# A two-layer decoder trunk: token-major first norm, query norm inside the softmax scale, later spreads and additions

## The chip, the cores and the metric

The kernel runs on one core of one Trainium2 chip. The metric is the device time of one execution in microseconds. Five engines work side by side: PE (TensorE, matrix products), DVE (VectorE), ACT (ScalarE), POOL (GpSimd) and SP, which here only issues DMAs. Each runs its own instructions in program order, and they wait for one another by semaphores.

## The reference

272 tokens (16 meta tokens and 256 inputs) of 1024 numbers go through two layers; all is float32.

```
h = rms_norm(r, g1);  proj = h @ w_in        # q_lat 384 | kv_lat 256 | k_pe 32 | dq | dk | dv 512 each | gates 2 x 1024
# branch A, 8 heads
c_q = rms_norm(q_lat);   q = c_q @ w_uq      # per head 64 + 32, rotary on the 32
c_kv = rms_norm(kv_lat); k, v = c_kv @ w_ukv # per head 64 + 64; k gets rotary(k_pe), 32, shared
out_a = (softmax(q k^T / sqrt(96), causal) v) @ w_o_mla
# branch B, 4 heads, two maps each, rotary on the first 16 of 64
p = softmax(q1 k1^T / 8) - lam * softmax(q2 k2^T / 8)   # lam from exp of two sums of products
out_b = rms_norm(p v) * (1 - lam_init) @ w_o_diff
r = r + rms_norm((sigmoid(g_a) * out_a + sigmoid(g_b) * out_b) @ w_out)
r = r + rms_norm((silu(gu[:2816]) * gu[2816:]) @ w_down),  gu = rms_norm(r) @ w_gate_up
```

The output is the residual stream without the meta tokens. A `rms_norm` divides by a root over a token's numbers, so its factor is one number per token and can be multiplied in after the matrix product.

## The kernel before, in words

Activations lie with features on the 128 partitions and tokens along the free axis, as 8 chunks of 128 x 272. Each float32 product is made of three: a value is split into a high part (a cast to fp32r, on ACT) and a low part (value minus high part, on DVE), and PE multiplies high by high, high by low and low by high. The inputs' chunks are `hh` and `hl`, the weights `w_hi` and `w_lo`.

Weights come as 252 slots of 128 x 1024 (512 KB) in the order of use. SP's `load` fills a ring of 4 raw slots, and waits for the low part of slot n - 4 before it loads slot n. ACT's `split` casts a raw slot into a ring of 8 high parts, DVE's `split` (L718) subtracts into a ring of 8 low parts. ACT runs 7 slots ahead of the tile that an instruction order is at, DVE 6. PE's `tile` does 24 matmuls for an output tile of 128 features (8 chunks x 3) into one of the PSUM banks: six up to the middle of the ukv tiles, four behind them. `bank_free` makes it wait until the tile that had the bank before is evacuated, which DVE counts in `tile_free`.

The order of every engine is written out by hand. In a layer, PE makes the latent tiles `lat` (6), `dq` and `dk` (4 each), then in turn the query tiles `uq` (6 short ones), `dv` (4) and key and value tiles `ukv` (8 short ones), then 16 `gate` tiles, between which the attention of 12 heads (units) stands, then `oa`, `ob`, `out`, the FFN's `gu` and `down`. After gate tile 2 come `keys_ready` and, in layer 0, `meta_rows` (the scores of the meta tokens); inside gate tile 3 the first scores; behind gate tile 4 the first `transposes` of probabilities.

A norm is done in steps. ACT squares chunk by chunk, POOL adds, PE's `norm_sums` multiply by a column of ones, ACT's `root` takes the root, DVE's `recip` the reciprocal, and PE's `spread` transposes the column of factors into rows across all partitions, from where DVE's `take` (L731) copies them. The first norm is squared from x while the first two slots are split in quarters (`quarter_split`), and its spread stands inside tile lat 3. The latents' norms are spread inside tile dk 1 (`latent_spreads`). The query norm's factors are multiplied in when DVE evacuates the uq tiles: with the rotary tables (`rcos_q`, `rsin_q`) for the rotary part, directly (L926) for the rest.

Rotary parts are two products, one of them moved along the partitions by a shuffle, and added on POOL (`rope_add`: 0 the shared key, 1 dq, 2 dk, 3 uq). ACT copies the rotary part of the queries into place (L468, "placing"). DVE makes the masks in bf16 and the product and sum for lambda after tile lat 3; ACT's exp and DVE's `lambdas` follow. `keep_clock` issues small matmuls on idle data, 50 of them at the start.

## Time and profile before

| | us |
|---|---|
| median of 3 runs (lowest, highest) | 828.0 (827.8, 829.01) |
| the profiled execution | 828.09 |
| its span | 826.1 |
| PE, DVE, ACT, POOL busy | 812.8, 590.5, 451.5, 128.8 |

The span runs from the first to the last instruction that the profile shows; what the profiled execution took beside it lies around it. Matmuls are pipelined, so PE's busy time includes the time in which one matmul's end overlaps the next one's start: the distance from start to start tells more than the duration.

### The profile page before, as it was taken

Reading aid. Unit: us, or ns where it says so; the run is one execution under the profiler, and the core shown is the slowest. Engines: PE = TensorE matmul, PEld = TensorE weight load, DVE = VectorE, ACT = ScalarE, POOL = GpSimd, SP = SyncE. Lnnn points to the kernel's source line nnn. Section 1 sums busy time; section 2 is a strip of 40 time slices with the busy share of each in tenths; the row PEclk is TensorE's granted clock in tenths of the full one; section 3 lists DMA queues with packets and bytes.
Section 4 is the critical chain, followed back from the end, with each engine's and each line's share of the span. In section 5 each row is a group of like instructions: output and inputs, shape, how many; then the busy total and the mean of one; then the engine's idle time right before and its main releaser. Section 6 shows DMA issues by size and latency. Waiting matters only on the chain.

```text
span 826.1 us, 17079 instructions
## 1 busy us (share of the span) xinstructions
PE 812.8 (98%) x6437; PEld 789.2 (96%) x6437; DVE 590.5 (71%) x1000; ACT 451.5 (55%) x749; POOL 128.8 (16%) x128
## 2 busy tenths in 40 slices
PE   8999999999999999999999999999999999999997
PEld 8999999999999999999999999899999999999885
DVE  4999586569588666666668996876787876766432
ACT  6755555475566444455556547554766655545431
POOL 2122000004341111101113220000054211111000
PEclk9999999999999999999999999999999999999999
DMA  7666523235527656446662666233363566555631
GB/s 288 215 193 203 158 78 103 80 100 182 176 74 251 182 159 180 129 144 186 178 201 81 202 196 210 80 102 102 105 229 102 184 226 188 182 189 177 205 102 51
DMA packets 38747, 131.59 MB, mean 159 GB/s; under 512 B 4384, under 2 KB 4768, under 8 KB 38688
## 3 DMA queue, kind: packets, MB, share of 16 engines
q1 hardware_dynamic: 38688, 130.77, 50.3%
q8 instruction: 42, 0.69, 0.3%
q14 instruction: 17, 0.14, 0.1%
HBM read 129.70 MB, written 1.05 MB: 158 GB/s over the span
## 4 chain that ended last, share of the span: by engine, by line
PE 81%; DVE 12%; ACT 2%; issue 2%; DMA 2%; POOL 0%; SPq 0%; DVEq 0%; POOLq 0%; ACTq 0%
PE bank L1147 20%; PE bank L1149 19%; PE bank L1148 19%; DVE w_lo L718 5%; PE bank L1183 4%; PE bank L1505 2%; PE bank L1506 2%; PE bank L1504 2%; PE bank L1172 2%; PE bank L1375 2%; DMA w_raw<-weights 2%; PE bank L1351 2%; PE bank L1390 1%; PE bank L1199 1%; ACT e_t L491 1%
## 5 line engine op out<-in xcount | busy, mean ns | idle before, releaser
L718 DVE TENSOR_TENSOR w_lo<-w_raw,w_hi 128x1024 fp32r<-128x1024 f32 x250 | 337.2, 1351 | 38.4 <-ACT w_hi L362 36.2
L1147 PE MATMUL bank<-h_hi,w_hi 128*128 128x272 f32 (+1 forms) x1232 | 357.8, 290 | 0.0
L1149 PE MATMUL bank<-h_hi,w_lo 128*128 128x272 f32 (+1 forms) x1232 | 352.0, 286 | 0.0
L1148 PE MATMUL bank<-h_lo,w_hi 128*128 128x272 f32 (+1 forms) x1232 | 351.2, 285 | 0.0
L362 ACT ACTIVATE w_hi<-w_raw 128x1024 fp32r<-128x1024 f32 x250 | 262.4, 1054 | 125.0 <-PE bank L1149 53.9
L1147 PEld LDWEIGHTS bank<-h_hi,w_hi 128*128 128x128 f32 x1232 | 232.0, 188 | 1.3 <-issue 0.2
L1149 PEld LDWEIGHTS bank<-h_hi,w_lo 128*128 128x128 f32 x1232 | 231.8, 188 | 0.0
L1148 PEld LDWEIGHTS bank<-h_lo,w_hi 128*128 128x128 f32 x1232 | 231.6, 188 | 0.0
L642 POOL TENSOR_TENSOR acc<-acc,sq 128x272 f32<-128x272 f32 (+1 forms) x51 | 52.5, 1029 | 143.6 <-ACT sq L375 143.1
L687 POOL TENSOR_TENSOR pbuf<-sbuf,ubuf 128x272 f32<-128x272 f32 (+1 forms) x44 | 38.7, 878 | 205.4 <-DVE ubuf L1081 203.8
L1081 DVE TENSOR_TENSOR ubuf<-bank,rstd_h 128x272 f32<-128x272 f32 (+1 forms) x44 | 18.9, 431 | 45.2 <-PE bank L1149 45.2
L1147 PE MATMUL bank<-ff_hi,w_hi 128*128 128x272 f32 x176 | 50.7, 288 | 0.0
L1149 PE MATMUL bank<-ff_hi,w_lo 128*128 128x272 f32 x176 | 50.6, 288 | 0.0
L1148 PE MATMUL bank<-ff_lo,w_hi 128*128 128x272 f32 x176 | 50.6, 287 | 0.0
L675 POOL TENSOR_TENSOR gates<-gates 128x272 f32<-128x272 f32 (+1 forms) x16 | 15.7, 1005 | 208.9 <-DVE gates L736 208.9
L591 ACT ACTIVATE sbuf<-gbuf 128x272 f32<-128x272 f32 (+1 forms) x44 | 18.7, 424 | 51.3 <-DVE gbuf L1081 51.0
L491 ACT ACTIVATE e_t<-bank,small 128x272 f32<-128x272 f32 x64 | 27.1, 431 | 31.0 <-DVE small L945 31.0
L1183 PE MATMUL bank<-h_hi,w_hi 128*128 128x272 f32 (+1 forms) x144 | 38.1, 293 | 2.8 <-DVE w_lo L787 2.4
L1183 PE MATMUL bank<-h_hi,w_lo 128*128 128x272 f32 (+1 forms) x144 | 37.7, 290 | 0.0
L1505 PE MATMUL bank<-w_lo,ff_hi 128*128 128x512 f32 x88 | 34.7, 395 | 0.0
L1506 PE MATMUL bank<-w_hi,ff_lo 128*128 128x512 f32 x88 | 34.7, 394 | 0.0
L1504 PE MATMUL bank<-w_hi,ff_hi 128*128 128x512 f32 x88 | 34.6, 394 | 0.0
(211 smaller groups left out, 1238.1 us busy)
## 6 DMA issues: line engine op xcount, KB each, us to landing
w_raw<-weights SPq DMA_DIRECT2D x220, 512.0 KB, 3.7
w_raw<-weights SPq DMA_DIRECT2D x16, 384.0 KB, 3.1
w_raw<-weights SPq DMA_DIRECT2D x16, 320.0 KB, 2.8
resid<-x_t SPq DMA_DIRECT2D x4, 272.0 KB, 5.3
out_tokens<-o_tok SPq DMA_DIRECT2D x4, 256.0 KB, 2.0
cst<-consts SPq DMA_DIRECT2D x1, 544.0 KB, 6.2
gain_bc<-gain_rows SPq DMA_DIRECT2D x1, 512.0 KB, 4.3
y<-consts SPq DMA_DIRECT2D x1, 256.0 KB, 5.8
```

Of the source, the lines that this page charges most:

```text
L362: act.activation(w_hi[:, n % RING, :], w_raw[:, n % RAW, :], ACT.Copy).then_inc(hi_ready, 1)
L491: last = act.activation(e_t[:, e, a:b], ps[bank][:, a:b], ACT.Exp, bias=mx[u % 2][:, s + part:s + part + 1], scale=scale, accum_out=sm[u % ...
L642: pool.tensor_tensor(acc[:, K % 2, t0:], acc[:, K % 2, t0:], sq[:, plan.sq_place[K, c], t0:], ALU.add).then_inc(sq_added, 1)
L687: pool.tensor_tensor(pbuf[:, j % 2, t0:], sbuf_[:, j % 2, t0:], ubuf[:, j % 2, t0:], ALU.mult).then_inc(ff_prod, 1)
L718: dve.tensor_tensor(w_lo[:, n % RING, :], w_raw[:, n % RAW, :], w_hi[:, n % RING, :].bitcast(f32), ALU.subtract).then_inc(lo_ready, 1)
L1147: pe.matmul(dst, wh, hi, start=first, stop=False)
L1148: pe.matmul(dst, wh, lo, start=False, stop=False)
L1149: return pe.matmul(dst, wl, hi, start=False, stop=last)
L1183: pe.matmul(ps[bank_of(t)][:, t0:TOK], w[:, n % RING, k * P:(k + 1) * P], src[k][0], start=k == 0 and q == 0, stop=False)
L1504: pe.matmul(dst, x_hi, wh, start=k == 0, stop=False)
L1505: pe.matmul(dst, x_hi, wl, start=False, stop=False)
L1506: return pe.matmul(dst, x_lo, wh, start=False, stop=k == FC - 1)
```

## The change

What it does, part by part:

- **First norm.** x is also passed token by token (`x_rows`). ACT squares and sums each token's row in one instruction with an accumulator, takes the root over 3 columns, and DVE the reciprocal; PE only spreads it (`first_spread`), inside tile lat 5. The 8 squares, POOL's additions and PE's 12 sums of this norm go.
- **First weights and inputs.** Slots 0 to 3 arrive in a buffer of their own in 5 pieces (by chunks of rows: 1, 1, 2, 2, 2), between the pieces of x; the gains come inside the first one. ACT and DVE split piece by piece. PE makes four tiles at once (`start_tiles`), per piece high by high, high by low input, low weights. 40 warm-up matmuls instead of 50. The first slot that waits for a ring place on SP is slot 8.
- **Query norm.** Its factor is no longer multiplied into the queries nor spread by PE. As it is a number per query, it goes into the softmax scale: `pscale` and `nscale`, a column each, in ACT's exp and DVE's negative maximum. ACT instead of DVE evacuates uq tiles 2 to 5, as plain copies.
- **Latent spread.** Only the key and value norm is spread, in tile dk 3 instead of dk 1.
- **Rotary additions.** `rope_add` 2 and 3 on POOL wait for the last ukv tile. ACT places the queries after the second v copy (gate tile 1) and not between the dv tiles.
- **Masks and lambda.** The casts of the masks go to POOL, at its start. Lambda's product and sum come at gate tile 0, exp at 1, `lambdas` at 3 (layer 0).

The diff, cut to its core:

```diff
@@ SP
+            for i, (a, b) in enumerate(PIECES):
+                if a % 2 == 0:
+                    xs = slice(GAIN_COLS + a * TOK if a else 0, GAIN_COLS + (a + 2) * TOK)
+                    sp.dma_start(x_sb[:, xs], xT[:, xs]).then_inc(x_in[a // 2], 16)
+                ws = slice(FIRST * P * a, FIRST * P * b)
+                sp.dma_start(w_first[:, ws], first_weights[:, ws]).then_inc(piece_in[i], 16)
+            load(4, SLOT)
+            load(5, SLOT)
             sp.dma_start(cst[:, 0:P], consts[:, 0:P]).then_inc(id_in, 16)
+            sp.dma_start(x_tok[:, 0:2, :], x_rows[:, 0:2 * D_MODEL].rearrange("p (c d) -> p c d", c=2)).then_inc(rows_in, 16)
+            sp.dma_start(x_tok[0:N_META, 2, :], x_rows[0:N_META, 2 * D_MODEL:]).then_inc(rows_in, 16)
+            load(6, SLOT)
...
@@ ACT
             first_hi(0, 1)
+            piece_split(0)
+            piece_split(1)
             first_hi(2, 3)
+            piece_split(2)
             first_hi(4, 5)
+            piece_split(3)
             first_hi(6, 7)
+            piece_split(4)
+            split(FIRST)
+            split(FIRST + 1)
+            act.wait_ge(rows_in, 32)
+            for c, (a, b) in enumerate(KEYS):
+                n = b - a
+                act.activation(x_sq[0:n, c, :], x_tok[0:n, c, :], ACT.Square, accum_out=x_sum[0:n, c:c + 1]).then_inc(row_squared, 1)
+            act.wait_ge(row_squared, len(KEYS))
+            act.activation(std[0][:, 0:len(KEYS)], x_sum, ACT.Sqrt, bias=eps, scale=1.0 / D_MODEL).then_inc(norm_std, 1)
...
                 for st, i in TURNS:
                     split(S(st, i) + HI_AHEAD)
-                    if (st, i) == ("dv", 2):
-                        act.wait_ge(rope_done, 4 * (l + 1))
-                        for q in range(4):
-                            act.activation(q_t[64:96, q::4, t0:], q_rot[32 * q:32 * q + 32, :, t0:], ACT.Copy).then_inc(q_placed, 1)
+                    if st == "uq" and i >= 1:
+                        for j in (2 * i, 2 * i + 1):
+                            t, h = TL("uq", j), 2 * j - 4
+                            act.wait_ge(pe_done, plan.tile_done[t])
+                            act.activation(q_t[0:NOPE, h, t0:], ps[bank_of(t)][0:NOPE, t0:TOK], ACT.Copy)
+                            act.activation(q_t[0:NOPE, h + 1, t0:], ps[bank_of(t)][NOPE:, t0:TOK], ACT.Copy).then_inc(act_free, 1)
...
                         if i < 3:
                             v_evac(i)
+                            if i == 1:
+                                act.wait_ge(rope_done, 4 * (l + 1))
+                                for q in range(4):
+                                    act.activation(q_t[64:96, q::4, t0:], q_rot[32 * q:32 * q + 32, :, t0:], ACT.Copy).then_inc(q_placed, 1)
+                            if i == 1 and l == 0:
+                                act.wait_ge(lam_ready, 1)
+                                act.activation(lam_e, lamp, ACT.Exp).then_inc(lam_exp, 1)
@@ POOL
-            sum_squares(0, 0)
+            pool.wait_ge(id_in, 16)
+            pool.wait_ge(mask_in, 16)
+            pool.wait_ge(pe_done, plan.tile_done[0])
+            pool.tensor_copy(identb[:, :], ident)
+            pool.tensor_copy(maskb[:, :], stage[:, 0, 0:P])
+            pool.tensor_copy(maskmb[:, 0:128], stage[0:16, 0, 128:256])
+            pool.tensor_copy(maskmb[:, 128:256], stage[0:16, 1, 0:128]).then_inc(const_ready, 1)
...
                 rope_add(l, 1, dqk[:, 0:4, t0:], rot["dq"][:, :, t0:])
+                pool.wait_ge(pe_done, plan.tile_done[plan.tile[l, "ukv", MLA_HEADS - 1]])
                 rope_add(l, 2, dqk[:, 4:8, :], rot["dk"])
                 rope_add(l, 3, q_rot[:, :, t0:], rot["uq"][:, :, t0:])
@@ DVE
+            for i, (a, b) in enumerate(PIECES):
+                dve.wait_ge(x_in[a // 2], 16)
+                for c in range(a, b):
+                    lo_part(0, c, G_MIXPRE, 0, 0)
+                piece_split(i)
+            split(FIRST)
+            split(FIRST + 1)
             recip(PRE_MIX, 0)
             take(PRE_MIX, 7, rstd_h, 0)
...
                         if st == "dq" and i == 3:
                             recip(K0 + NQ, t0)
+                            query_scales(K0 + NQ, len(token_chunks(t0)))
                             recip(K0 + NKV, 0)
-                        if st == "dk" and i == 1:
-                            take(K0 + NQ, 7, rstd_q, t0)
+                        if st == "dk" and i == 3:
                             take(K0 + NKV, 6, rstd_kv, 0)
-                            v = step(dve.tensor_tensor(rc_q[:, t0:], rstd_q[:, t0:], cos_m[:, t0:], ALU.mult))
-                            v = step(dve.tensor_tensor(rs_q[:, t0:], rstd_q[:, t0:], sin_m[:, t0:], ALU.mult))
...
-                        dve.tensor_scalar(mx[u % 2][:, s:s + 2], mx[u % 2][:, s:s + 2], -scale, None, ALU.mult).then_inc(negmax_ready, 1)
+                            dve.tensor_tensor(mx[u % 2][:, s:s + 2], mx[u % 2][:, s:s + 2], nscale, ALU.mult).then_inc(negmax_ready, 1)
...
                         split(S("gate") + i + AHEAD)
+                        if i == 0 and l == 0:
+                            lambda_sums()
                         if i == 3 and l == 0:
+                            lambdas()
@@ PE
+            def start_tiles(src):
+                for i, (a, b) in enumerate(PIECES):
+                    for k in range(a, b):
+                        pe.wait_ge(h_hi, k + 1)
...
+                            pe.wait_ge(piece_hi, i + 1)
+                        for t in range(FIRST):
+                            pe.matmul(ps[t][:, :TOK], w_hi[:, t, k * P:(k + 1) * P], src[k][0], start=k == 0, stop=False)
+                    for k in range(a, b):
+                        pe.wait_ge(h_lo, k + 1)
+                        for t in range(FIRST):
+                            pe.matmul(ps[t][:, :TOK], w_hi[:, t, k * P:(k + 1) * P], src[k][1], start=False, stop=False)
...
+                        pe.wait_ge(piece_lo, i + 1)
+                    for k in range(a, b):
+                        for t in range(FIRST):
+                            mm = pe.matmul(ps[t][:, :TOK], w_lo[:, t, k * P:(k + 1) * P], src[k][0], start=False, stop=k == KC - 1)
...
-            keep_clock(50)
+            keep_clock(40)
...
+                first_norm = {4: first_spread} if l == 0 else {0: lambda: norm_sums(K0 + PRE_MIX, 7, 0), 4: lambda: norm_spread(K0 + PRE_MIX, 7, 0)}
                 for i in range(4, 6):
                     slot_ready(S("lat") + i)
+                    tile(TL("lat") + i, S("lat") + i, 0, P if i < 5 else HW, full, 0, inside=first_norm if i == (4 if l else 5) else None)
                 def latent_spreads():
-                    norm_spread(K0 + NQ, 7, t0)
-                    norm_spread(K0 + NKV, 6, 0)
+                    pe.wait_ge(norm_rec, K0 + NKV + 1)
+                    spread(K0 + NKV, 6, 0, count=2)
...
-                        tile(TL(st) + i, S(st) + i, 0, P, src, c0, inside={6: latent_spreads} if (st, i) == ("dk", 1) else None)
+                        tile(TL(st) + i, S(st) + i, 0, P, src, c0, inside={6: latent_spreads} if (st, i) == ("dk", 3) else None)
```

Where a tile's evacuation was counted in `tile_free` alone, the counts are now kept per engine (`emptied`, with `act_free` for ACT's). Buffers move a little in SBUF; the computation is the same.

## Rows read from the trace of the kernel before

**Rows 1.** Page, part 1: busy us, share of the span, instructions.

```profile
...
PE 812.8 (98%) x6437; PEld 789.2 (96%) x6437; DVE 590.5 (71%) x1000; ACT 451.5 (55%) x749; POOL 128.8 (16%) x128
...
```

**Rows 2.** Timeline, all engines, start: start us, us, engine line op tiles, [idle before].

```profile
...
1.06 4.63 PE L1225 MATMUL bank<-identb 128*128 128x128 bf16 x50 [1.06 <-DVE identb L780]
...
4.11 0.93 ACT L401 ACTIVATE h_hi<-resid,gain 128x272 fp32r<-128x272 f32 x2 [1.87 <-DMA resid<-x_t]
...
6.70 1.15 ACT L407 ACTIVATE w_hi<-w_raw 128x512 fp32r<-128x512 f32 x2 [1.66 <-DMA w_raw<-weights]
...
8.11 0.60 PE L1183 MATMUL bank<-h_hi,w_hi 128*128 128x272 f32 x1 [2.42 <-DVE w_lo L787]
...
```

**Rows 3.** Windows: PE, PEld, DVE, ACT, POOL busy (instructions); granted clock; DMA share, GB/s.

```profile
...
4.60:8.00 3.40, 1.09 (x19) 0.92 (x17) 1.55 (x4) 1.74 (x5) 0.00 (x0) 1.00 1.01 318
8.00:11.40 3.40, 3.29 (x14) 3.29 (x15) 3.12 (x7) 3.40 (x9) 0.77 (x1) 0.50 1.04 407
22.00:86.00 64.00, 62.50 (x493) 61.65 (x493) 61.50 (x110) 40.13 (x53) 13.47 (x10) 1.00 0.67 205
...
```

**Rows 4.** Waits of PE, whole span: total us, times, longest.

```profile
...
PE bank L1218 <- DVE small L726: 2.4, 2, 1.2
...
```

**Rows 5.** Timeline of PE, four short stretches.

```profile
...
18.73 0.72 PE L1199 MATMUL bank<-small,acc 128*128 128x1 f32 x6
...
19.99 0.37 PE L1147 MATMUL bank<-h_hi,w_hi 128*128 128x272 f32 x1
...
23.55 0.29 PE L1147 MATMUL bank<-h_hi,w_hi 128*128 128x272 f32 x1
...
79.35 0.29 PE L1149 MATMUL bank<-h_hi,w_lo 128*128 128x272 f32 x1
79.94 0.36 PE L1147 MATMUL bank<-lat_hi,w_hi 128*128 128x272 f32 x1 [0.30 <-DVE kv_t L736]
...
499.48 0.28 PE L1149 MATMUL bank<-lat_hi,w_lo 128*128 128x272 f32 x1
499.90 0.39 PE L1147 MATMUL bank<-lat_hi,w_hi 128*128 128x272 f32 x1
...
```

**Rows 6.** Timeline of DVE, layer 0 up to the gates.

```profile
...
22.99 0.44 DVE L731 COPY rstd_h<-bank 128x272 f32<-128x272 f32 x1 [0.63 <-PE bank L1218]
...
32.55 0.21 DVE L805 CAST identb<-cst 128x128 bf16<-128x128 f32 x1
...
40.59 0.16 DVE L818 TENSOR_TENSOR small<-small 128x1 f32<-128x1 f32 x1
...
52.80 2.92 DVE L718 TENSOR_TENSOR w_lo<-w_raw,w_hi 128x1024 fp32r<-128x1024 f32 x1
...
69.84 0.43 DVE L926 TENSOR_TENSOR q_t<-bank,rstd_q 64x272 f32<-64x272 f32 x1
...
```

**Rows 7.** Timeline of POOL, layer 0 up to the gates.

```profile
...
51.30 3.34 POOL L651 TENSOR_TENSOR dqk_t<-dqk_t,b_t 128x1088 f32<-128x1088 f32 x1 [8.82 <-DVE b_t L897]
63.31 3.37 POOL L651 TENSOR_TENSOR dqk_t<-dqk_t,gates 128x1088 f32<-128x1088 f32 x1 [8.67 <-DVE gates L897]
68.98 2.17 POOL L651 TENSOR_TENSOR gates<-gates 128x544 f32<-128x544 f32 x1 [2.29 <-DVE gates L908]
...
```

**Rows 8.** Timeline of ACT, end of ukv and gates of layer 0.

```profile
...
74.85 2.70 ACT L468 ACTIVATE q_t<-gates 32x544 f32<-32x544 f32 x4
...
95.53 0.90 ACT L483 ACTIVATE v_tok<-bank 128x256 f32<-128x256 f32 x3 [2.23 <-PE bank L1307]
...
97.40 1.28 ACT L516 ACT_TABLE_LOAD   x1
...
```

**Rows 9.** Timelines of DVE (two rows) and PE, gates of layer 0.

```profile
...
96.94 0.41 DVE L990 TENSOR_REDUCE small<-bank 16x16 f32<-16x256 f32 x1 [0.69 <-PE bank L1329]
...
103.94 0.78 DVE L967 SCALAR_TENSOR_TENSOR e_t<-e_t,small 128x272 f32<-128x272 f32 x2
...
105.08 0.71 PE L1375 MATMUL bank<-cst,e_t 128*128 128x128 f32 x5
...
```

More of the change, by code:

```diff
@@ L129, in __init__ @@
         self.slots = len(self.slot_done)
+        self.emptied, counts = [], {}
+        for t, (l, name) in enumerate(self.name_of):
+            by = "act" if name == "uq" and t - self.tile[l, name, 0] >= 2 else "dve"
+            counts[by] = counts.get(by, 0) + 1
+            self.emptied.append((by, counts[by]))
         self.bank, self.before = [], []
@@ L150, in __init__ @@
             for k in range(NORMS):
-                if k in CHUNKS:
+                if k in CHUNKS and (l or k != PRE_MIX):
                     K = l * NORMS + k
@@ L158, in __init__, with build_trunk @@
                         self.sq_free[K, c] = users[-2] if len(users) >= 2 else None
-                        users.append(("sum", K + 1) if last else ("add", a))
+                        users.append(("sum", K) if last else ("add", a))
                     s += CHUNKS[k]
-def build_trunk(nc: bass.Bass, xT, weights, gains, lam_in, consts, gain_rows, out):
+def build_trunk(nc: bass.Bass, xT, x_rows, first_weights, weights, lam_in, consts, gain_rows, out):
     f32, f32r, bf16 = mybir.dt.float32, mybir.dt.float32r, mybir.dt.bfloat16
@@ L666, in _ @@
                 pool.wait_ge(rope_done, 4 * (l + 1))
-                pool.wait_ge(pe_done, plan.tile_done[plan.tile[l, "ukv", MLA_HEADS - 1]])
                 if l == 0:
@@ L1158, in tile, with first_tiles @@
                 mm.then_inc(pe_done, 1)
-            def first_tiles(tiles, ready, before=None):
+            def first_tiles(tiles, ready):
                 if tiles[0][1]:
@@ L1177, in first_tiles @@
                 for k in range(KC):
-                    if before and k in before:
-                        before[k]()
                     pe.wait_ge(hi_sem, base + k + 1)
@@ L1247, in _ @@
                 if l == 0:
-                    first_tiles([(TL("lat") + q, S("lat") + q, late, t0) for q in range(2)], (h_hi, h_lo, 0),
-                                {0: lambda: pe.wait_ge(quarter_lo, 1), 2: lambda: pe.wait_ge(quarter_lo, 2),
-                                 4: lambda: pe.wait_ge(quarter_lo, 3), 6: lambda: slot_ready(1)})
-                    slot_ready(S("lat") + 2)
-                    tile(TL("lat") + 2, S("lat") + 2, 0, P, late, t0)
-                    norm_sums(K0 + PRE_MIX, 7, 0)
-                    pe.wait_ge(id_in, 16)
-                    slot_ready(S("lat") + 3)
-                    tile(TL("lat") + 3, S("lat") + 3, 0, P, full, 0, inside={6: lambda: norm_spread(K0 + PRE_MIX, 7, 0)})
+                    start_tiles(full)
                 else:
@@ L1296, in v_transposes @@
                         pe.wait_ge(norm_ready, K0 + NKV + 1)
-                        pe.wait_ge(tile_free, TL("dv", 3) + 1)
+                        emptied(pe, TL("dv", 3))
+                        for b in range(BANKS, BANKS + EXTRA):
+                            emptied(pe, max(t for t in range(TL("gate")) if plan.bank[t] == b))
                     else:
-                        pe.wait_ge(tile_free, TL("ukv", 4 * g - 1) + 1)
+                        emptied(pe, TL("ukv", 4 * g - 1))
                         pe.wait_ge(v_copied, 9 * l + 3 * g)
@@ L1624 @@
     gain_rows = np.broadcast_to(A(norm_ffn_post)[DEPTH - 1][None, :], (P, D_MODEL))
-    arrays = {"x_t": x_t, "weights": packed, "gains": gains, "lam": lam, "consts": constants(), "gain_rows": gain_rows}
+    first = packed[0:FIRST * P].reshape(FIRST, P, SLOT)
+    first = np.concatenate([first[:, :, a * P:b * P].transpose(1, 0, 2).reshape(P, -1) for a, b in PIECES], axis=1)
+    arrays = {"x_t": x_t, "x_rows": x_rows, "first_weights": first, "weights": packed, "lam": lam, "consts": constants(), "gain_rows": gain_rows}
     arrays = {k: np.ascontiguousarray(v) for k, v in arrays.items()}
```

221 lines of the change are left out of this document (112 added, 109 removed).

## The prediction, made before the changed kernel ran

> **What bounds the kernel now.** I read the page first: PE is busy 812.8 of 826.1 us [rows 1]. A busy PE says little by itself, so I looked at what PE waits for and at the distance between its matmul starts: from 8.11 us on, matmuls of 272 columns start 0.125 us apart almost without a break. So time is won only where PE's stream starts earlier, waits less or gets shorter. There are three such places.
>
> The start: the warm-up matmuls are issued by 5.5 us, the first useful one runs at 8.11, after 2.42 us idle [rows 2]. Behind it the granted clock is 0.50, the 1.2 GHz level, from 8.0 to 11.4; in the stretch before, PE was busy 1.09 of 3.4 us [rows 3].
>
> The latent spread: PE waits 1.2 us twice, once a layer, for DVE's reciprocal [rows 4].
>
> The bank of a ukv tile: ukv 4 starts at 79.94, after 0.30 us of waiting for an evacuation by DVE [rows 5]. DVE is busy 61.5 of the 64 us from 22 to 86 [rows 3] and has fallen behind PE by then: it is second in line, and a gain of PE ahead of this point is worth nothing unless DVE gets shorter too.
>
> **The start.** The fourth tile ends and the fifth begins at 23.55 now [rows 5]. Call that moment E. Landings: x's first piece (272 KB behind 38 KB of gains) is there at 4.1, the first half of two slots (0.84 MB in all) at 6.7 [rows 2]; from 8.0 on 407 GB/s flow [rows 3]. By these, and with SP's first issue now x itself (0.3 us saved), 0.58 MB (x and piece 0) are there at 5.0, 0.84 at 6.35, 1.65 at 8.35, 2.45 at 10.35 and 3.25 MB (piece 4) at 12.3. To cast 512 columns takes ACT 0.6 us (two took 1.15 [rows 2]), 1024 take 1.05; with the h_hi casts between them the high parts end at 5.7, 7.0, 9.5, 11.5 and 13.4. PE has 12 matmuls for each of eight row chunks, 96 x 0.125 = 12.0 us. It starts at 5.75, runs chunks 0 and 1 to 8.75, waits 0.75 for piece 2, and then always has work: E = 5.75 + 12.0 + 0.75 = 18.5. The low part no longer stands ahead of the first matmul; DVE makes it in 0.65 us, while PE has 8 high matmuls. Gone are the cold stretch and the 12 column sums of the first norm with the wait at their end (18.73 to 19.99 [rows 5]). So E comes 5.05 us earlier. Bounds: 17.8 (no wait for pieces) and 20.5 (each landing 0.7 later, and the low clock once). The 10 warm-up matmuls that go end before PE could start, so they give nothing.
>
> The new norm: the token rows (1.1 MB) stand behind slots 4 and 5, 5.4 MB in all, so at some 17.6. Three squares on ACT at about 1.1 with their accumulator reads, and a root, give 21.6, the reciprocal 21.8. PE asks for it in the sixth tile, chunk 4, at E + 4.5 = 23.0: 1.2 to spare. A straggling DMA queue would use this up; bounds 0 and 1 us, I take 0.
>
> A new wait: slot 6's low part stands on DVE behind this later norm. Spread (0.33), copy and evacuation (0.35 each), and a split of 1.2 end at E + 7.1; PE is through the sixth tile at E + 6.3 and waits 0.8. Bounds 0.3 and 2.0 (the casts on POOL fall into it).
>
> **From there to ukv 4.** Now this takes 79.94 - 23.55 = 56.4 us. Off: the latent spread's wait 1.2 [rows 4], and 0.46 at ukv (79.35 to 79.94 less one pitch [rows 5]). The query norm's three transposes leave, the first norm's three come in. On: 0.8. So 55.5, if DVE keeps up. The spread itself: DVE's reciprocals come at E + 28.7, PE asks in dk 3, chunk 6, at E + 31.7; two tiles earlier it would wait.
>
> DVE's own sum: its chain began with the copy at 22.99 [rows 6], now at E + 5.0 = 23.5, 0.5 later. It loses four casts 0.55, the lambda product and sum 0.78, the lambda steps 1.26, the copy of the query factor 0.34, two rotary products 0.7, and eight query evacuations 3.7 (0.43 each and their gaps) [rows 6]: 7.3 us. Four small operations for the scales add 0.6. The evacuation that PE waited for would be ready at 79.9 + 0.5 - 6.7 = 73.7; PE arrives at 18.5 + 55.5 = 74.0. They meet. But a split in this chain took 2.92 instead of 1.2: it ended 1.1 behind the end of a POOL addition (51.30 + 3.34 [rows 6, 7]). The second addition, dk's at 63.31 [rows 7], held up another split by 1.0; it now runs after the last ukv tile. That puts DVE 1.3 us ahead.
>
> The Trainium skill, "SBUF — State Buffer", Who interferes with whom, has this as a lock: a DVE instruction with two SBUF inputs and a POOL one that reads SBUF exclude each other, and the first one holds it for its whole length. By that rule the trace agrees. It also speaks against the casts and additions on POOL, which by it may stand behind a split or hold up one.
>
> ACT takes the eight query copies (0.43 each, 3.4 us) and gives up the placings (2.70 [rows 8]), one exp and one sqrt table load (1.28 each) in this stretch, in which it is busy 40 of 64 us [rows 3]: nothing. The banks that they free are asked for six tiles later, 1.8 us to spare.
>
> So PE reaches ukv 4 at 74.0, 5.9 us earlier.
>
> **The gates of layer 0.** Here is a loss. In the old clock times: the last v copies run at 95.53 after 2.23 us idle [rows 8]; ahead of them now stand the four placings (2.7) and the exp of lambda with its table load (1.5). They end at 98.3, and the scores start at 98.5: just no wait. But ACT's split of that turn ends 4 us later, DVE's behind it at 98.6, then come the lambda steps (1.25), and the meta maxima start at 99.9 instead of 96.94 [rows 9]. The table load that held up the meta exp (97.40 [rows 8]) is done by then: 0.9 back. So the first probabilities, ready at 104.72 now, come 2.1 later; PE, which takes them up at 105.08 [rows 9], had 0.3 to spare. Loss 1.8; bounds 0.5 (DVE's split isn't late) and 2.6. POOL's two additions (3.37 and 2.17 [rows 7]) end at 88.8, ACT asks at 92.3: 3.5 to spare.
>
> **Layer 1.** Spread wait 1.2, two transposes 0.2, ukv wait 0.3 (499.48 to 499.90 less a pitch [rows 5]): 1.7 off. The placings sit between the v copies here too, and the scores start where the copies end: 0.1 on. What follows the gates, the FFNs and the tail are untouched and bound by PE; they move along.
>
> **Sum.** 5.9 - 1.8 + 1.7 - 0.1 = 5.7 us. The profiled execution took 828.09 (span 826.1 and 2.0 around it), the median of the three is 828.0, so they are one: 822.4 us.
>
> **Rivals.** A: the clock. If PE's gaps of 0.4 us before its start and of 0.75 at 8.8 bring back the 1.2 GHz level for as long as now, 3.4 us [rows 3], PE loses half of that, less what it idles anyway: 1.5, so 823.9. For it: a gap did so now. Against: that one was 2.42 us. The Trainium skill, "TensorE: Matmul & The Clock Gate", Part 1, says that activity releases the clock and idling takes it back.
>
> B: DVE or ACT sets the pace up to ukv. DVE's lead is 0 to 1.3 us, and it hangs on slot 6's late split and on ACT's order, in which a query copy waits behind a split that waits for a load. If they are 3 us short, PE gives back 3: 825.4.
>
> C: no loss at the gates, and the pieces land at their best: 5.7 + 1.8 + 0.7 = 8.2, 819.9.
>
> D, slower: POOL's additions between the last ukv tile and the keys. The attention of a layer now waits for a chain: 5.5 us of additions, then four placings of 2.7, in order on ACT. If splits and additions shut each other out so that the additions end 7.5 us later than alone (13 for 5.5), the 3.5 to spare are used up and PE waits 4 in each layer: 822.4 + 8.0 = 830.4. It makes the kernel slower from a wait of 2.9 per layer on. For it: the split of 2.92. Against: one split of 1.2 ahead of each addition is only 2.4 of the 3.5.
>
> **Chances.** The forecast (821 to 823.4) 0.50, A 0.14, B 0.17, C 0.12, D 0.05, no change at all 0.02. The range is 819.4 (C with half a microsecond more) to 825.9 (B and a late norm). A measurement tells 0.2%, 1.7 us, from no change, so faster is under 826.3: forecast, A and C are faster, B mostly. Faster 0.87, same 0.08, slower 0.05.
>
> **What would show it.** The first useful matmul at 5.7 to 6.0 and the clock at 1.00 from there; the fifth tile at 18.5; a new wait of 0.8 for a low part before dq 0; no wait at the latent spreads; no doubled split beside the dk addition; ukv 4 at 74; a wait of about 1.8 before the first transposes of layer 0, with the meta maxima late. The forecast is wrong if the fifth tile starts after 20.5, if PE waits for key or query placings, or if over 3 us of PE waits appear between dq 0 and the first transposes.

## The result and the profile after

| | before | after |
|---|---|---|
| median of 6 runs each (lowest, highest) | 828.3 (827.8, 829.01) | 821.98 (821.15, 822.15) |
| the profiled execution | 828.09 | 822.15 |
| its span | 826.1 | 820.4 |

The ratio of the two is 0.9923, with a 95% interval from 0.9913 to 0.9933: the kernel became 0.8% faster, 0.4 us away from the forecast of 822.4. The profiled execution after is the slowest of its six. In the tables below "after" is the median of 821.98. The same kernel before, timed again beside each group of experiments, gave 828.08 to 828.18, so the groups can be set against each other.

The page and the windows of after, which answer to [rows 1, 3]. Columns of the windows: busy time (instructions) of each engine, then granted clock, DMA share, GB/s.

```profile
PE 809.3 (99%) x6410; PEld 786.1 (96%) x6410; DVE 583.9 (71%) x981; ACT 459.1 (56%) x760; POOL 122.3 (15%) x126
```

```profile
4.60:8.00 3.40, 3.40 (x25) 3.21 (x24) 2.42 (x5) 2.19 (x5) 0.00 (x0) 1.00 0.95 333
8.00:11.40 3.40, 2.40 (x19) 2.20 (x19) 1.99 (x4) 2.36 (x5) 0.00 (x0) 1.00 1.03 409
22.00:86.00 64.00, 63.14 (x506) 62.41 (x505) 59.04 (x95) 41.19 (x61) 13.72 (x14) 1.00 0.67 216
```

From 8.0 to 11.4 us the granted clock is 1.00 where it was 0.50, and PE works from 4.6 to 8.0 where it was idle for 2.42 us [rows 2, 3]. (The clock's record begins at 6.59 us in this trace, and the view counts what lies ahead of it as 1.00; the last section comes back to this.) DVE has 59.0 us of work in the 64 where it had 61.5. What PE waits for in the whole execution (total, times, longest):

```profile
PE bank L1439 <- DVE e_t L1004: 1.4, 4, 0.6
PE bank L1295 <- DVE identb L820: 1.1, 1, 1.1
PE bank L1237 <- ACT w_hi L430: 1.0, 1, 1.0
PE bank L1187 <- DVE w_lo L757: 0.6, 1, 0.6
PE bank L1405 <- DVE pm L1043: 0.6, 1, 0.6
PE bank L1187 <- DVE gates L775: 0.2, 1, 0.2
```

The two waits for DVE's `small` [rows 4] are gone. New are one for the first pieces (L1237), one for a low part (L1187), one for a bank in the query tiles (L1187, `gates`), one for the meta probabilities (L1405), and 0.65 of the 1.4 us at L1439. These are gaps between matmuls; from start to start, less the usual 0.125, a wait comes out 0.1 to 0.2 us longer, and the text counts it so: 1.17, 0.80, 0.38 and, at the gates, 0.65 and 0.8. PE's timeline shows their places:

```profile
1.09 4.45 PE L1295 MATMUL bank<-identb 128*128 128x128 bf16 x40 [1.09 <-DVE identb L820]
5.49 1.24 PE L1237 MATMUL bank<-h_hi,w_hi 128*128 128x272 f32 x4
6.53 0.69 PE L1241 MATMUL bank<-h_lo,w_hi 128*128 128x272 f32 x4
...
10.25 1.00 PE L1237 MATMUL bank<-h_hi,w_hi 128*128 128x272 f32 x6 [1.00 <-ACT w_hi L430]
...
19.37 0.29 PE L1187 MATMUL bank<-h_hi,w_hi 128*128 128x272 f32 x1
...
26.53 0.39 PE L1187 MATMUL bank<-h_hi,w_hi 128*128 128x272 f32 x1 [0.64 <-DVE w_lo L757]
...
74.97 0.29 PE L1187 MATMUL bank<-lat_hi,w_hi 128*128 128x272 f32 x1
...
97.62 0.76 PE L1405 MATMUL bank<-cst,pm 16*16 16x16 f32 x24 [0.57 <-DVE pm L1043]
...
101.48 0.77 PE L1439 MATMUL bank<-cst,e_t 128*128 128x128 f32 x5 [0.65 <-DVE e_t L1004]
```

Where PE stands against before (the first matmul of each place):

| place in PE's order | before | after | earlier by |
|---|---|---|---|
| fifth tile (E) [rows 5] | 23.55 | 19.37 | 4.18 |
| ukv 4 [rows 5] | 79.94 | 74.97 | 4.97 |
| first probabilities of layer 0 [rows 9] | 105.08 | 101.48 | 3.60 |
| start of layer 0's FFN | 225.78 | 221.77 | 4.01 |
| start of layer 1 | 430.36 | 426.44 | 3.92 |
| start of layer 1's FFN | 631.95 | 625.82 | 6.13 |
| first matmul of 512 columns | 759.23 | 753.11 | 6.12 |
| the end of the span | 826.1 | 820.4 | 5.7 |

### The profile page after: what moved, and what is told of

Read it like the earlier page. It is cut to its first block, busy times and chain, and to the rows that moved or that the text cites. A ratio compares the mean times of both kernels' runs of the same rounds, so it can differ in the third digit from the quotient of the medians.

```text
span 820.4 us, 17023 instructions
## 1 busy us (share of the span) xinstructions
PE 809.3 (99%) x6410; PEld 786.1 (96%) x6410; DVE 583.9 (71%) x981; ACT 459.1 (56%) x760; POOL 122.3 (15%) x126
## 4 chain that ended last, share of the span: by engine, by line
PE 90%; DVE 6%; ACT 2%; issue 1%; DMA 1%; SPq 0%; POOL 0%; DVEq 0%; POOLq 0%
PE bank L1187 22%; PE bank L1189 22%; PE bank L1188 22%; PE bank L1221 4%; PE bank L1568 3%; PE bank L1570 2%; PE bank L1569 2%; DVE w_lo L757 2%; PE bank L1212 2%; PE bank L1439 2%; PE bank L1415 1%; PE bank L1454 1%; PE bank L1269 1%; ACT e_t L515 1%; DMA w_first<-first_weights 1%
## 5 line engine op out<-in xcount | busy, mean ns | idle before, releaser
L1187 PE MATMUL bank<-h_hi,w_hi 128*128 128x272 f32 (+2 forms) x1216 | 353.1, 290 | 0.6 <-DVE w_lo L757 0.6
L1189 PE MATMUL bank<-h_hi,w_lo 128*128 128x272 f32 (+2 forms) x1216 | 347.4, 286 | 0.0
L1188 PE MATMUL bank<-h_lo,w_hi 128*128 128x272 f32 (+2 forms) x1216 | 346.6, 285 | 0.0
L1187 PEld LDWEIGHTS bank<-h_hi,w_hi 128*128 128x128 f32 (+1 forms) x1216 | 229.0, 188 | 1.9 <-DVE w_lo L757 0.9
L1189 PEld LDWEIGHTS bank<-h_hi,w_lo 128*128 128x128 f32 (+1 forms) x1216 | 228.8, 188 | 0.0
L1188 PEld LDWEIGHTS bank<-h_lo,w_hi 128*128 128x128 f32 (+1 forms) x1216 | 228.7, 188 | 0.0
L674 POOL TENSOR_TENSOR acc<-acc,sq 128x272 f32<-128x272 f32 (+1 forms) x45 | 46.9, 1042 | 124.7 <-ACT sq L399 124.7
L1187 PE MATMUL bank<-ff_hi,w_hi 128*128 128x272 f32 x176 | 50.7, 288 | 0.0
L515 ACT ACTIVATE e_t<-bank,small 128x272 f32<-128x272 f32 x64 | 30.0, 476 | 29.9 <-DVE small L982 18.2
L1187 PEld LDWEIGHTS bank<-ff_hi,w_hi 128*128 128x128 f32 x176 | 33.2, 189 | 0.0
L1188 PEld LDWEIGHTS bank<-ff_lo,w_hi 128*128 128x128 f32 x176 | 33.2, 188 | 0.0
```

What stands on the lines that cost most here:

```text
L515: last = act.activation(e_t[:, e, a:b], ps[bank][:, a:b], ACT.Exp, bias=mx[u % 2][:, s + part:s + part + 1], scale=scale, accum_out=sm[u % ...
L674: pool.tensor_tensor(acc[:, K % 2, t0:], acc[:, K % 2, t0:], sq[:, plan.sq_place[K, c], t0:], ALU.add).then_inc(sq_added, 1)
L1187: pe.matmul(dst, wh, hi, start=first, stop=False)
L1188: pe.matmul(dst, wh, lo, start=False, stop=False)
L1189: return pe.matmul(dst, wl, hi, start=False, stop=last)
```

## The experiments

Each was made from the changed kernel by the edit shown. Times are medians, with the lowest and highest run behind them.

| run | us | against after |
|---|---|---|
| spread_dk1 | 828.92 (828.05 to 830.95) | +6.9 |
| two_halves | 827.47 (825.86 to 828.76) | +5.5 |
| halves_warm50 | 827.75 (826.49 to 828.13) | +5.8 |
| halves_spread_dk1 | 835.31 (834.75 to 836.59) | +13.3 |
| norm_by_chunks | 824.47 (823.97 to 826.93) | +2.5 |
| uq_on_dve | 824.37 (823.55 to 824.58) | +2.4 |
| adds_early | 822.89 (822.28 to 823.09) | +0.9 |
| adds_place_early | 822.64 (822.19 to 823.01) | +0.7 |
| slot6_early | 822.05 (821.22 to 822.88) | +0.1 |
| warm50 | 821.83 (821.70 to 822.18) | -0.2 |
| gates_and_slot6 | 820.62 (820.14 to 821.20) | -1.4 |
| gates_order | 820.14 (819.87 to 822.70) | -1.8 |

### The latent spread: spread_dk1

```diff
-inside={6: latent_spreads} if (st, i) == ("dk", 3) else None
+inside={6: latent_spreads} if (st, i) == ("dk", 1) else None
```

(and DVE's `take` of it with it.)

> The changed kernel, with only the latent spread put back from tile dk 3 to tile dk 1 in both layers. My theory: the earlier start and the later spread need each other. In layer 0 PE now asks in dk 1, chunk 6, at about 45.4 us, and DVE's second reciprocal is ready at 49.4: a wait of 4.0. In layer 1 it is 1.3 as before the change. PE is the bound behind it, so nothing is given back: 5 us slower than the changed kernel, 827.0 (826 to 828). Rival: DVE is second in line, so while PE waits DVE catches up and the waits of 0.4 at uq and 1.5 at the gates shrink or go: 3.5 slower, 825.5. Second rival: the spread's move hides nothing that matters, under 1 us: 822.5.

Measured: 828.92, ratio to before 1.0007 (0.9996 to 1.0018). This edit alone takes back all of the gain, more than my theory or a rival said. PE's longest waits, its timeline at the spread, and the windows around it:

```profile
PE bank L1288 <- DVE small L765: 5.5, 2, 3.8
```

```profile
44.60 0.29 PE L1189 MATMUL bank<-h_hi,w_lo 128*128 128x272 f32 x1
48.73 0.54 PE L1288 MATMUL bank<-cst,small 128*128 128x128 f32 x3 [3.84 <-DVE small L765]
...
49.48 0.43 PE L1187 MATMUL bank<-h_hi,w_hi 128*128 128x272 f32 x1
49.71 0.43 PE L1188 MATMUL bank<-h_lo,w_hi 128*128 128x272 f32 x1
```

```profile
44.00:48.60 4.60, 0.89 (x8) 0.67 (x6) 4.57 (x14) 3.03 (x4) 0.00 (x0) 1.00 0.84 245
48.60:53.00 4.40, 4.27 (x22) 4.27 (x23) 4.40 (x7) 3.25 (x4) 2.76 (x1) 0.61 0.65 192
```

PE idles 4.0 us in layer 0 and 1.85 in layer 1. Behind the first wait matmuls start 0.23 us apart instead of 0.125, at the 1.2 GHz level, for 3.4 us: that costs another 1.5. Waits further down (0.38 before the uq tiles) go in exchange. Together 7.0; between the profiled executions it is 6.3, as this one's fifth tile starts 0.64 earlier (18.73). In layer 1 the wait was 1.33 before the change, and why it is 0.5 longer now stays open: the first norm of that layer wasn't touched.

### The start: two_halves, and both together

```diff
-PIECES = [(0, 1), (1, 2), (2, 4), (4, 6), (6, 8)]
+PIECES = [(0, 4), (4, 8)]
```

(the casts follow the pieces.)

> The first weight stage and the input are fetched in two halves of four chunks again, with the casts on ScalarE and VectorE half by half, and the matmuls in two rounds; the rest stays as changed. My theory: the first useful matmul comes at about 8.1 us instead of 5.5 and the end of the fifth tile at about 23.2 instead of 19.4, and, with the spread late, all of that goes through to the end: 825.9 us (824.8 to 827.0). Rival (the later start is taken up by the waits behind it, since VectorE's norm then is ready earlier against TensorE and the waits at 25.6 and in the gates go too): 823.5 to 824.7. Second rival (the pieces are worth nothing, all is the spread and the norm): 822.0 to 822.5.

Measured: 827.47; the profiled run was the lowest, 825.86. ScalarE's timeline there, and in halves_warm50, a profiled run of the common kind:

```profile
6.97 1.91 ACT L430 ACTIVATE w_hi<-w_first 128x2048 fp32r<-128x2048 f32 x1 [1.51 <-DMA w_first<-first_weights]
```

```profile
9.31 1.91 ACT L430 ACTIVATE w_hi<-w_first 128x2048 fp32r<-128x2048 f32 x1 [3.77 <-DMA w_first<-first_weights]
```

The trace's landing records show why they differ: 15 of the 16 DMA engines had brought the first 1 MB by 6.93 us in one and by 7.02 in the other; the sixteenth came at 6.95 and at 9.29. In the profiled run everything behind the start is the changed kernel's, 3.8 us later (the fifth tile starts at 23.15 instead of 19.37, the matmul behind the wait for slot 6's low part at 30.30 instead of 26.53), and the span is 3.7 longer. So a microsecond at the start is one at the end, as my theory had it; the forecast of 825.9 held for that run but not for the median. The next run asks whether the clock is the cause.

```diff
-keep_clock(40)
+keep_clock(50)
```

> The two halves of the run two_halves, with 50 warm-up matmuls instead of 40, as the kernel before had. The profiled run of two_halves took 825.9 us, but most of its others 827.3 to 828.8. My theory: TensorE sits idle there for 3.8 us ahead of its first useful matmul, so in most runs the clock falls back for some us; ten more warm-up matmuls shorten the idle time to about 2.7 us, and the time is 825.9 us (825.2 to 827.0), with nearly all runs there. Rival (the idle time is still long enough, as in the kernel before, whose records show 0.50 from 8.0 to 11.4): 827.4 (827.0 to 828.2).

Measured: 827.75, all but one of 11 runs above 827. It is the rival's number, but the clock isn't what sets this run apart from the faster one. The late sixteenth engine makes PE idle 5.6 us, and the first matmuls then run at the 1.2 GHz level:

```profile
8.00:11.40 3.40, 0.03 (x1) 0.06 (x1) 0.14 (x1) 2.09 (x2) 0.00 (x0) 0.52 1.00 400
11.40:15.00 3.60, 3.60 (x16) 3.60 (x17) 3.60 (x5) 3.20 (x5) 0.00 (x0) 0.50 1.04 426
```

They did so in the profiled run of two_halves too, whose record of the clock begins only at 13.65 us: its first 16 matmuls take 3.8 us, as long as here.

```profile
9.03 3.96 PE L1234 MATMUL bank<-h_hi,w_hi 128*128 128x272 f32 x16 [3.50 <-ACT w_hi L430]
12.79 2.55 PE L1238 MATMUL bank<-h_lo,w_hi 128*128 128x272 f32 x16
```

PE works at that level for 4.6 us there (9.03 to 13.65) and for 3.6 here (11.37 to 14.98), so the clock costs about 2 us in both. What differs is when the first matmul starts, 9.03 and 11.37, and the fifth tile, 23.15 and 25.05: that is the late engine, and it covers the 1.76 us between the two executions. There is one trace of each, so whether it also made the other runs of two_halves long isn't shown.

The third has two_halves' and spread_dk1's edits together.

> Two halves at the start and the latent spread back in tile dk 1, both at once: the start is as late as before, the first norm is the new one. My theory: the later latent spread is needed because the first norm now is spread 4.4 us behind the end of the fifth tile instead of ahead of it, so that VectorE's chain stands some 5 us further behind TensorE than before, whatever the start; then TensorE waits 3 to 4 us for the reciprocals in layer 0 and 1.9 in layer 1 here too, and the time is 833.0 us (831.0 to 835.0), slower than the kernel before. Rival (the spread wait of 4.0 us in spread_dk1 came from the earlier start alone: VectorE's reciprocal comes at its own time, 48 to 50 us, and a start 3.8 us later takes the wait back to about 1): 828.5 us (827.5 to 830.0).

Measured: 835.31, ratio 1.0082 (1.0068 to 1.0096), slower than before, and 2.3 above what I expected. The wait is as long as in spread_dk1, though the fifth tile starts 7.3 us later (25.99):

```profile
PE bank L1285 <- DVE small L762: 5.6, 2, 3.9
```

The clock costs more here than in spread_dk1. PE's first matmul starts at 11.30, as in halves_warm50, and it runs at the 1.2 GHz level up to 17.10; behind the wait of 4.0 us the level is 0.50 until 61.48, twice as long as in spread_dk1, and costs 2.5 us instead of 1.5:

```profile
54.60:61.40 6.80, 5.38 (x24) 5.38 (x25) 6.77 (x15) 4.88 (x4) 3.30 (x1) 0.50 0.69 231
```

So the wait doesn't come from the early start. By the timelines it comes from the place of the first norm's spread; no run moved that spread alone. Before, it stood inside the fourth tile, and DVE's chain began with the copy at 22.99, 0.56 ahead of E [rows 5, 6]. Now it stands in the sixth, and DVE's chain begins here in the changed kernel, 5.06 behind E:

```profile
22.89 0.18 DVE L765 RECIPROCAL small<-small 128x3 f32<-128x3 f32 x1 [4.71 <-ACT small L452]
24.43 0.44 DVE L770 COPY rstd_h<-bank 128x272 f32<-128x272 f32 x1 [1.36 <-PE bank L1256]
...
48.65 0.17 DVE L765 RECIPROCAL small<-small 128x3 f32<-128x3 f32 x1
```

DVE's chain starts 5.6 us later against E than before, and has lost 2.6 us of work by then (four casts, lambda): 3.0, against a wait that grew by 2.6. In spread_dk1 PE reaches the spread 26.0 us behind E and goes on 30.0 behind it. Two tiles (6 us) later, where the change puts it, there is no wait.

### The first norm: norm_by_chunks, slot6_early, warm50

The first norm of before, in the changed kernel (edit cut to its core):

```diff
-            sp.dma_start(x_tok[:, 0:2, :], x_rows[...]).then_inc(rows_in, 16)
...
-                act.activation(x_sq[0:n, c, :], x_tok[0:n, c, :], ACT.Square, accum_out=x_sum[0:n, c:c + 1]).then_inc(row_squared, 1)
+            for c in range(KC):
+                square(0, c, r[:, c, :], 0)
+            root(0, 7, D_MODEL, 0)
...
+            sum_squares(0, 0)
```

> The first norm is that of the kernel before again (squares chunk by chunk on ScalarE, added on GpSimd, summed over the partitions by TensorE in tile 5, no token-major rows fetched); the fetch pieces, the later latent spread, the query norm in the softmax scale and the rest stay as changed. My theory: the three sums of TensorE come back (0.15 to 0.25 us) and the squares share ScalarE with the casts of the pieces, whose reciprocal then comes a little later or earlier than 22.9; 822.8 us (822.2 to 823.6), so that the token rows are worth 0.8 of the 6.3 us. Rival (the rows and their fetch of 4 KB per token compete with the pieces and delay the fifth tile): without them the pieces land earlier and the time is 821 to 821.8. Second rival (the norm comes late by chunks and TensorE waits at the first spread): 824.5 or more.

Measured: 824.47, by the second rival's number; 823.97 in the profiled run, 1.8 above that of after, and all of it stands ahead of 28.3 us (the matmul behind the wait for the low part starts there at 28.32 instead of 26.53). PE's matmuls from 12 to 30 us (busy, mean ns), POOL's chain, and the wait for it:

```profile
L1265 PE MATMUL bank<-small,sq 128*128 128x1 f32 x6 | 0.8, 250 | 0.0
L1265 PE MATMUL bank<-small,acc 128*128 128x1 f32 x6 | 0.8, 249 | 0.7 <-POOL acc L669 0.7
```

```profile
16.92 5.73 POOL L669 TENSOR_TENSOR acc<-acc,sq 128x272 f32<-128x272 f32 x6 [16.47 <-ACT sq L397]
```

12 sums at 0.11 from start to start are 1.3 us, and 0.9 is waited for POOL, whose last addition ends at 22.65; a fifth tile that starts 0.5 earlier (18.90) takes a part back. I had left the 12 sums out of that expectation's price, though not out of the prediction's.

```diff
             recip(PRE_MIX, 0)
+            split(AHEAD)
             take(PRE_MIX, 7, rstd_h, 0)
```

(and the same split leaves its old place, behind the first evacuation.)

> VectorE's low part of the first slot of the latent stage's second group is moved ahead of the first norm's take, right behind the reciprocal; one statement is moved, nothing else. My theory: the 0.80 us that TensorE waits for that low part at 25.60 goes, and as much as 0.2 comes in at the first spread, whose take now ends later: 821.4 us (821.1 to 821.8). Rival (VectorE's whole load sets the pace up to the keys' and values' first tile): the 0.8 us come again at the next low parts or at the normalized chunks, and the time is that of the changed kernel, 822.0 (821.8 to 822.3).

Measured: 822.05, the rival's number. The wait before dq 0 falls only from 0.80 to 0.38 us, as DVE's split now waits 0.77 us for ACT's high part, and 0.7 us come again as waits before a uq tile (0.52 at 63.09; 0.38 was there) and a ukv tile (0.55 at 71.28).

> 50 warm-up matmuls instead of 40, nothing else. By the prediction's step the ten end before TensorE could start anyway. But the trace of the changed kernel shows the 40 ending right at the first useful matmul (5.49 us), so ten more, at about 0.11 us each, push it back. My theory: first useful matmul at 6.6, but the wait for piece 2 at 8.9 swallows what comes before it; time 822.0 us (821.6 to 822.5). Rival (the matmuls up to there are then late against piece 2 by more than the wait): 823.0. Second rival (the full clock from the first matmul on is worth something, the first ones being 0.26 us apart now): 821.3.

Measured: 821.83, no change that can be told. Here the full clock came only at 6.61 us, so the ten more matmuls took 1.06 us and pushed the first useful one from 5.49 to 6.36. But the trace has a fifth tile that starts at 18.62 instead of 19.37, and this in the sixth:

```profile
6.36 0.86 PE L1237 MATMUL bank<-h_hi,w_hi 128*128 128x272 f32 x4
...
23.61 0.40 PE L1256 MATMUL bank<-cst,small 128*128 128x128 f32 x2 [0.30 <-DVE small L765]
```

Piece 2 landed at 8.17 instead of 9.03, and PE, which came 0.5 us later, found it there. That isn't the edit's doing: in adds_place_early, with 40 matmuls, piece 2 landed at 8.17 too and the fifth tile starts at 18.52. Of the 0.75 us gained 0.48 is waited at the first norm's spread, since the last token rows land no earlier (19.67, and 19.27 in the changed kernel). An earlier start than the changed kernel's is worth next to nothing as long as the norm isn't earlier too.

### DVE's reserve: uq_on_dve, adds_early, adds_place_early

```diff
-by = "act" if name == "uq" and t - self.tile[l, name, 0] >= 2 else "dve"
+by = "dve"
```

(and the eight copies with it.)

> The changed kernel, with the evacuation of query tiles 2 to 5 back on DVE (plain copies, no factor), in both layers. My theory: up to the ukv tiles DVE is as late as PE. Eight copies of 0.43 put 3.4 us back on it per layer; its reserve at ukv is some 1.5 to 2 us in the trace of the changed kernel (it idles 0.9 ahead of slot 26's split and 0.2 elsewhere). PE then waits 1.5 to 2.5 us for banks in uq and ukv in layer 0 and 0 to 1 in layer 1: 824.2 (823 to 825.5). Rival: DVE has real slack and ACT was no help: under 0.5 us, 822.2.

Measured: 824.37, as expected. The eight copies (3.4 us of DVE) return as waits of 2.0 us, the longest of them here, and none in layer 1:

```profile
PE bank L1187 <- DVE q_t L962: 0.9, 1, 0.9
```

```diff
-                pool.wait_ge(pe_done, plan.tile_done[plan.tile[l, "ukv", MLA_HEADS - 1]])
                 rope_add(l, 2, dqk[:, 4:8, :], rot["dk"])
                 rope_add(l, 3, q_rot[:, :, t0:], rot["uq"][:, :, t0:])
                 pool.wait_ge(rope_done, 4 * (l + 1))
+                pool.wait_ge(pe_done, plan.tile_done[plan.tile[l, "ukv", MLA_HEADS - 1]])
```

> The changed kernel, with the rotary additions of dk and uq on POOL back ahead of the last ukv tile, in both layers; the placing of the queries stays late. My theory: a split of DVE beside the dk addition doubles again (2.2 in place of 1.2) and takes 1.0 of DVE's reserve of about 1.5 before ukv, and the long split (2.68) and the long lambda product (1.57) beside the additions in gate tile 0 go, where DVE has time. So no change of time: 822.0 (821.6 to 822.6). Rival: DVE's reserve is used up and PE waits 1 us per layer: 823.5 to 824. Second rival: the additions in the gates hold up the chain to the keys, and it gets 1 us faster: 821.

Measured: 822.89, 0.9 above the changed kernel, where I expected none: the reserve was smaller than I took it for. There is a new wait of 0.79 us before a dv tile (66.14), as the addition now stands beside DVE's splits again (one took 2.17); the waits at the gates stay.

The fourth takes the placings back between the dv tiles as well.

> The changed kernel, with the additions of dk and uq as before the change and the four placings of the queries on ACT back between dv 2 and ukv, in both layers. My theory: the loss at the gates of layer 0 (waits of 0.65 ahead of the meta transposes and 0.8 ahead of the first transposes) comes from ACT's order: placings 2.7 and lambda's exp 1.5 ahead of the third split and v copy. Without the placings there, ACT and DVE reach the meta maxima 1.3 to 2.4 us earlier and the waits shrink to 0 to 0.3. On the other side ACT spends 2.7 more ahead of ukv, where a split of DVE waited 0.9 for it. Net 0.5 to 1.4 faster than the changed kernel: 821.0. Rival: the loss comes from DVE's lambda steps alone (1.25), so it stays: 822.0. Second rival: ACT is late at ukv and PE waits there: 823 or more.

Measured: 822.64, and not the gain that I expected. The waits at the gates, 0.65 and 0.8 us, do go, but 0.8 is waited before a dv tile (66.08) and 0.9 before a ukv tile (78.49) instead. Both additions and placings stand better where the change puts them.

### The gates of layer 0: gates_order, gates_and_slot6

ScalarE and VectorE in the changed kernel at the gates. The order is: placings, table load, exp of lambda, a split, the v copies; VectorE waits for that split, makes the lambda steps and only then the meta maxima (L1030).

```profile
87.32 2.70 ACT L542 ACTIVATE q_t<-gates 32x544 f32<-32x544 f32 x4
90.04 1.28 ACT L545 ACT_TABLE_LOAD   x1
91.33 0.20 ACT L545 ACTIVATE small<-small 128x4 f32<-128x4 f32 x1
91.44 1.04 ACT L386 ACTIVATE w_hi<-w_raw 128x1024 fp32r<-128x1024 f32 x1
```

```profile
92.52 1.23 DVE L757 TENSOR_TENSOR w_lo<-w_raw,w_hi 128x1024 fp32r<-128x1024 f32 x1 [2.46 <-ACT w_hi L386]
...
94.42 0.41 DVE L1030 TENSOR_REDUCE small<-bank 16x16 f32<-16x256 f32 x1
```

```diff
 ACT
-                        split(S("gate") + i + HI_AHEAD)
+                        if i < 3 or l:
+                            split(S("gate") + i + HI_AHEAD)
...
-                            if i == 1 and l == 0:
-                                act.wait_ge(lam_ready, 1)
-                                act.activation(lam_e, lamp, ACT.Exp).then_inc(lam_exp, 1)
...
+                            act.wait_ge(lam_ready, 1)
+                            act.activation(lam_e, lamp, ACT.Exp).then_inc(lam_exp, 1)
                             act.wait_ge(meta_shift, 1)
...
+                            split(S("gate") + i + HI_AHEAD)
 DVE
-                            lambdas()
...
+                            lambdas()
                             dve.wait_ge(meta_exp, 1)
```

> In layer 0's gates, the lambda exponential and the meta exponential stand on ScalarE ahead of its high-part copy of gate 3, and VectorE's lambda steps behind the shift of the meta scores; nothing else. My theory: in the changed kernel the two waits of TensorE there (0.65 and 0.8 us) hang on that order: VectorE's low part at 92.52 waits 2.46 us for ScalarE's high part, which stands behind the placings, the table load and the exponential, and the steps behind it push the meta probabilities back. With the order mended both go, and the time is 820.5 us (820.0 to 821.2), 1.5 below the changed kernel. Rival (VectorE's total sets the pace here, as the run with the placing brought forward hints): the waits come again in front of the first scores tile, 821.6 to 822.0. Second rival (the split, now later, holds the last gate): a wait of 1 to 2 us at gate tile 3, 823.

Measured: 820.14, ratio to before 0.9909 (0.9895 to 0.9923), four of five runs at or below 820.42. The split comes at 89.75 there, and the maxima 2.4 us earlier:

```profile
90.83 1.22 DVE L758 TENSOR_TENSOR w_lo<-w_raw,w_hi 128x1024 fp32r<-128x1024 f32 x1 [1.06 <-ACT w_hi L386]
91.98 0.40 DVE L1030 TENSOR_REDUCE small<-bank 16x16 f32<-16x256 f32 x1
```

Both waits are gone from PE's list: 1.45 of the 1.73 us between the two profiled executions. This is the best version of the study, though its interval and the changed kernel's still overlap; that the gain is real rests on the trace as well.

> The order of gates_order and the low part moved of slot6_early, both. My theory after those two runs: VectorE's total up to the last key and value tile sets when TensorE gets there, so the low part gives nothing by itself and nothing here: 820.2 us (819.8 to 820.8), the time of gates_order. Rival (with the gates mended a gain ahead of them is kept): 819.5.

Measured: 820.62. The low part gives nothing here either.

## Why the prediction was right, step by step

- **The start.** Forecast E = 18.5, measured 19.37. The first useful matmul ran at 5.49 (forecast 5.75), but the first four were 0.26 us apart; the two first pieces took 3.5 us and not 3.0. Piece 2 was there at 9.03 (forecast 8.35), and PE waited 1.17 us instead of 0.75. So the sum was 0.87 too good in this run. The slow first matmuls cost nothing by themselves, as PE waited for piece 2 behind them. In the other nine traces with five pieces the fifth tile starts at 18.52 to 19.20 and piece 2 lands at 8.17 to 8.85, so the forecast sits at the lower edge of what was measured.
- **The warm-up.** The prediction said that the ten matmuls less end before PE could start anyway. They would not have: 40 of them end at 5.54, with the first useful one at 5.49, and 50 end at 6.60 in warm50. It cost nothing, because the wait for piece 2 lies behind it.
- **The new norm.** The step that was wrong without showing in the time: the rows were there at 19.3, not 17.6, and the reciprocal at 22.89, not 21.8. By the landing records the 1 MB of the first 256 tokens was complete at 17.11, in time; what came at 19.27 were the last 16 rows, 64 KB behind it in the queue (17.61 and 18.94 in uq_on_dve). ACT waits for both. To fetch the 16 rows first wasn't tried. With E 0.87 late there was no wait (the spread stands at 23.90, the reciprocal ends at 23.07). With E at 18.5 the 1.2 us "to spare" would have been none, and PE would have waited here, as it does for 0.48 in warm50.
- **The wait before dq 0**: forecast 0.8, measured 0.80.
- **From E to ukv 4**: forecast 55.5, measured 55.60. No wait at the spread or at ukv, but 0.38 us before a uq tile (63.47), where the forecast had none. DVE's lead was judged well: no large wait, but no reserve either, as uq_on_dve, adds_early and slot6_early show. A split beside the dq addition took 2.86 us (1.22 alone), as before [rows 6, 7]; at gate tile 0 another took 2.68 beside dk's, where nothing waits for it.
- **What the late spread is worth.** The prediction counted 1.2 us a layer off and said that two tiles earlier PE would wait, but not how long: 4.0 and 1.85 us, and 1.5 for the clock. The part of the change that looks like 2.4 us is the one on which all of it hangs.
- **The gates of layer 0**: forecast a loss of 1.8 by way of ACT's late split, DVE's low part and the meta maxima. Measured 0.65 + 0.8 = 1.45 by that way; maxima at 94.42, by the forecast's clock 99.4 instead of 99.9. gates_order shows that it is this chain.
- **Layer 1**: forecast 1.6, measured 2.2 (from 3.92 to 6.13 earlier). A stall of 0.41 us at 117.31 in layer 0 went too, which the prediction had not seen. The tail gave 0.4 back: the 264 matmuls of 512 columns take 61.40 us from the first start to the last and not 61.02. They do so in the traces of all the variants, so it belongs to the change and isn't scatter; what slows them is open.
- The sum: 4.2 + 0.8 - 1.4 + 0.3 + 2.2 - 0.4 = 5.7 by the spans, 5.94 between the profiled executions, forecast 5.7. The errors nearly cancel: E and the uq wait, -1.2; the tail, -0.4; layer 1 and the stall, +1.0; the gates, +0.4. The terms were each right to a microsecond; that the total is right to 0.4 us is luck.

The rivals. A, the clock: not in this kernel, where it didn't fall back at gaps of 1.17 and 0.8 us, but it did where PE had waited 4 us. The Trainium skill, "TensorE: Matmul & The Clock Gate", Part 1, says that idling takes the fast clock back; by that rule, the traces agree. B, DVE sets the pace: true to 0.4 us, and the reason why slot6_early gives nothing. C, no loss at the gates: real, but only with another order. D, late additions: they ended at 83.0 and ACT took them up at 87.32, with 4.3 us to spare.

## What to carry to other kernels

When the start is moved ahead, list what is now ready at its own time (a landing, a norm) and measure every later consumer against it: the gain is kept only if the first such consumer is moved back in the order too. Two parts of a change can each be worth nearly the whole gain; undo them one by one and together before you say which one did it. In an in-order engine, put a table load or another step that nobody awaits behind the cast for which another engine waits.

## What the runs showed of the hardware that was not expected

- One of 16 DMA engines can be 2.3 us late, and it then holds up a whole transfer of 1 MB: 9.29 instead of 7.02 us in halves_warm50. It was still 2.0 us behind in the 512 KB transfers after that. In the runs with five pieces the last engine was 0.0 to 0.9 us behind the fifteenth in the weight transfers up to 16 us. Pieces of 1 MB aren't needed for it: the kernel before has none, and in a transfer of its own that lands at 17.28 the last engine is 1.7 us behind. What makes it late stays open.
- A transfer of 64 KB right behind one of 1 MB landed 1.1 to 2.8 us after it, though it is 0.2 us of data at the 409 GB/s of this stretch.
- The granted clock that the views show is not a record at the very start. The trace's list of clock levels begins with its first entry, at 6.59 us in the changed kernel, and a window counts what lies ahead as 1.00. Up to there the matmuls start at half the pace: the 128-column warm-up ones 0.107 us apart, against 0.056 later, and the first four useful ones 0.227 (the first 0.365) against 0.125. In the kernel before both change at 4.60. So at the start the spacing of the matmuls tells the level.
- With the same warm-up from 1.1 us on, the full pace came at 4.6 to 7.1 us in the traces in which PE then had work. In two_halves and halves_spread_dk1 it had not come when the 40 warm-up matmuls ended at 5.53; PE idled 3.5 and 5.8 us and then worked at the 1.2 GHz level, until 13.65 and 17.10.
- A wait of 4.0 us in mid-kernel cost 5.5, by 3.4 us at the 1.2 GHz level behind it, in spread_dk1; the same wait cost 6.5 in halves_spread_dk1, where the level lasted 6.8. In both, the one of 1.85 in layer 1 cost only itself.
